# Differential attention stage: scores in two PSUM places instead of three, transposed groups in two banks instead of one

## The reference, cut to what matters

```
sc = einsum('bqhmd,bkhmd->bhmqk', q, k) * scale         # 4 heads, m = 0, 1, q and k of 32 dims
p  = softmax(where(key_chunk <= query_chunk, sc, -inf)) # chunks of 64 frames
a  = p[:, :, 0] - lam * p[:, :, 1]                      # difference of the two maps
o  = a @ v                                              # v of 64 dims
y  = rmsnorm(o) * g * (1 - lambda_init) * silu(gate)
```

## Time and profile before

| | us |
|---|---|
| median of 3 runs | 2056.37 (2056.11 to 2059.1) |
| the profiled execution | 2055.35 |
| its span, first to last instruction | 2053.6 |
| PE busy | 1873.9 (91%) |
| DVE busy | 1306.2 (64%) |
| ACT busy | 1083.0 (53%) |
| POOL busy | 604.1 (29%) |
| mean granted TensorE clock | 0.945 |

### The profile page before, as it was taken

How to read it: one execution, slowest core, us unless ns; L and a number is a source line. 1 busy time by engine, 2 the same in 40 slices (tenths; PEclk the granted TensorE clock), 3 DMA queues, 4 the chain that set the end, 5 groups by cost and what they waited for, 6 DMA issues and landing times.

```text
span 2053.6 us, 34304 instructions
## 1 busy us (share of the span) xinstructions
PE 1873.9 (91%) x11552; PEld 1579.8 (77%) x11552; DVE 1306.2 (64%) x2685; ACT 1083.0 (53%) x2406; POOL 604.1 (29%) x542
## 2 busy tenths in 40 slices
PE   6999998899999999999999959999788999989998
PEld 6999998678787878787878857777566666767886
DVE  7705887577777777777676832434477788754444
ACT  6321211566666666666666722433378989962221
POOL 0000000344444444444444500101145666650000
PEclk9999999999999999999999868999689999998999
DMA  6432113000010101010101021424710404016542
GB/s 217 105 72 62 66 66 108 13 8 25 7 25 6 26 5 26 5 26 5 26 5 26 4 75 56 130 74 131 169 28 16 98 18 99 7 39 234 181 144 82
DMA packets 121867, 129.29 MB, mean 63 GB/s; under 512 B 81936, under 2 KB 94992, under 8 KB 120464
## 3 DMA queue, kind: packets, MB, share of 16 engines
q1 hardware_dynamic: 121744, 127.86, 21.5%
HBM read 85.89 MB, written 41.94 MB: 62 GB/s over the span
## 4 chain that ended last, share of the span: by engine, by line
PE 68%; DVE 15%; issue 7%; ACT 5%; DMA 2%; POOL 2%; SPq 0%; DVEq 0%; POOLq 0%; ACTq 0%
PE ps L662 8%; PE ps L648 6%; PE ps L616 5%; PE ps L617 5%; PE ps L618 5%; PE ps L603 4%; PE ps L604 4%; PE ps L605 4%; DVE small L1503 4%; PE ps L896 3%; PE ps L897 3%; PE ps L898 3%; PE ps L636 2%; PE ps L637 2%; DVE ring L1363 2%
## 5 line engine op out<-in xcount | busy, mean ns | idle before, releaser
L1621 POOL TENSOR_TENSOR ring_r<-ring,sp_hi 128x512 fp32r<-128x512 f32 (+1 forms) x320 | 358.5, 1120 | 822.4 <-DVE sp_hi L1366 822.4
L662 PEld LDWEIGHTS ps<-v,ring 128*128 128x128 f32 x2176 | 298.8, 200 | 55.4 <-DVE acc L1383 22.8
L662 PE MATMUL ps<-v,ring 128*128 128x65 f32 x2176 | 298.2, 279 | 16.5 <-DVE acc L1383 10.2
L1009 ACT ACTIVATE ring<-ps 128x512 f32<-128x512 f32 (+1 forms) x320 | 170.5, 533 | 221.6 <-PE ps L637 165.6
L1363 DVE SCALAR_TENSOR_TENSOR ring<-ring,ps 128x512 f32<-128x512 f32 (+1 forms) x320 | 192.0, 600 | 34.8 <-ACT ring L1014 32.8
L603 PE MATMUL ps<-w_hl,ht_hi 128*128 128x256 f32 x768 | 213.5, 278 | 0.7 <-DVE w_hl L1244 0.6
L604 PE MATMUL ps<-w_hl,ht_hi 128*128 128x256 f32 x768 | 213.3, 278 | 0.0
L605 PE MATMUL ps<-w_hl,ht_lo 128*128 128x256 f32 x768 | 213.3, 278 | 0.0
L616 PE MATMUL ps<-ht_hi,w_hl 128*128 128x512 f32 x448 | 200.0, 446 | 13.3 <-DVE ring L1351 7.0
L1647 POOL TENSOR_TENSOR p<-p 128x1024 f32<-128x1024 f32 (+4 forms) x96 | 164.9, 1729 | 159.5 <-ACT p L1156 159.2
L1021 ACT ACTIVATE ring<-ps 128x512 f32<-128x512 f32 (+1 forms) x320 | 170.3, 532 | 60.5 <-PE ps L648 59.7
(11 more groups left out here) (186 smaller groups left out, 3954.3 us busy)
## 6 DMA issues: line engine op xcount, KB each, us to landing
w_raw<-in_w_narrow SPq DMA_DIRECT2D x18, 512.0 KB, 3.9
xb<-in_x SPq DMA_DIRECT2D x16, 512.0 KB, 4.1
gate_scr<-ring SPq DMA_DIRECT2D x64, 128.0 KB, 1.8
qk_scr<-w_hl SPq DMA_DIRECT2D x32, 256.0 KB, 3.4
gb<-gate_scr SPq DMA_DIRECT2D x16, 512.0 KB, 3.8
yb<-y_scr SPq DMA_DIRECT2D x16, 512.0 KB, 4.7
xr<-in_x SPq DMA_DIRECT2D x16, 512.0 KB, 4.3
out_y<-ob SPq DMA_DIRECT2D x16, 512.0 KB, 2.9
```

Source lines behind the costliest of these rows:

```text
L662: mm = pe.matmul(ps[:, 4 + i % 2, j * (HD + 1):(j + 1) * (HD + 1)], ring[:, 4 + i % 2, j * P:(j + 1) * P], v1[:, kb, :], start=True, stop= ...
L1621: nc.gpsimd.tensor_tensor(ring_r[:, i % 4, j0 * P:], ring[:, i % 4, j0 * P:], sp_hi[:, i % 4, j0 * P:].bitcast(F32), ALU.subtract).then_in ...
```

## The change

Three places in one edit: the scores use places j % 2 (banks 0 to 3) and TensorE waits for the exponential of the unit two before; the transposed groups alternate between banks 4 and 5 and wait for the copy of the group two before; the turn-back keeps bank 6 to itself and waits for VectorE's reading of the turn-back before.

```diff
         def df_ps(j):
-            return psf[:, (j % 3) * KEYS:(j % 3 + 1) * KEYS]
+            return psf[:, (j % 2) * KEYS:(j % 2 + 1) * KEYS]
...
-                if U >= 3:
-                    pe.wait_ge(df_e, U - 2)
+                if U >= 2:
+                    pe.wait_ge(df_e, U - 1)
                 for g in range(-(-keys // TQ)):
                     w = min(TQ, keys - g * TQ)
-                    mm = pe.matmul(ps[:, 2 * (j % 3) + g, 0:w], df_q[u][:, m, row * P:(row + 1) * P],
+                    mm = pe.matmul(ps[:, 2 * (j % 2) + g, 0:w], df_q[u][:, m, row * P:(row + 1) * P],
                                    df_k[u][:, m, first + g * TQ:first + g * TQ + w], start=True, stop=True)
                 if first + keys == (row + 1) * P:
-                    mm = pe.matmul(ps[:, 2 * (j % 3) + g, w - P:w], ident_b[:], df_mask_qk[:], start=False, stop=True,
+                    mm = pe.matmul(ps[:, 2 * (j % 2) + g, w - P:w], ident_b[:], df_mask_qk[:], start=False, stop=True,
                                    skip_group_check=True)
...
                 pe.wait_ge(df_a, 3 * s + (1 if end <= 8 else 2 if end <= big else 3))
-                if g == 0 and s >= 3 and s % 2:
-                    pe.wait_ge(df_ob, (s - 1) // 2)
-                elif G:
-                    wait_evac(G - 1)
+                if G >= 2:
+                    wait_evac(G - 2)
                 for n in range(GROUPS[g]):
-                    mm = pe.transpose(ps[:, 6, n * P:(n + 1) * P], p1[:, s % 3, ...], ident[:])
+                    mm = pe.transpose(ps[:, 4 + G % 2, n * P:(n + 1) * P], p1[:, s % 3, ...], ident[:])
...
                 pe.wait_ge(df_oc, b + 1)
-                wait_evac((2 * b + 3) * N_GR - 1 if 2 * b + 3 <= N_SL else N_SL * N_GR - 1)
+                pe.wait_ge(df_ob, b)
...
-                nc.scalar.activation(at[:, G % 3, 0:w], ps[:, 6, 0:w], ACT.Copy).then_inc(df_at_a, 1)
+                nc.scalar.activation(at[:, G % 3, 0:w], ps[:, 4 + G % 2, 0:w], ACT.Copy).then_inc(df_at_a, 1)
...
-                nc.vector.tensor_copy(at[:, G % 3, 0:w], ps[:, 6, 0:w]).then_inc(df_at_d, 1)
+                nc.vector.tensor_copy(at[:, G % 3, 0:w], ps[:, 4 + G % 2, 0:w]).then_inc(df_at_d, 1)
```

More of the change, by code:

```diff
@@ L825, in df_turn @@
                 pe.wait_ge(df_a, 3 * s + (1 if end <= 8 else 2 if end <= big else 3))
-                if g == 0 and s >= 3 and s % 2:
-                    pe.wait_ge(df_ob, (s - 1) // 2)
-                elif G:
-                    wait_evac(G - 1)
+                if G >= 2:
+                    wait_evac(G - 2)
                 for n in range(GROUPS[g]):
-                    mm = pe.transpose(ps[:, 6, n * P:(n + 1) * P], p1[:, s % 3, (first + n) * P:(first + n + 1) * P], ident[:])
+                    mm = pe.transpose(ps[:, 4 + G % 2, n * P:(n + 1) * P], p1[:, s % 3, (first + n) * P:(first + n + 1) * P], ident[:])
                 mm.then_inc(df_t, 1)
```

## The result

The changed kernel takes 2240.26 us, median of 4 runs (2232.22 to 2255.99), against 2057.73 for the kernel before in the same comparison: ratio 1.0898, 95% interval 1.0871 to 1.0925. Forecast were 2257 us with a range of 2165 to 2345. The profiled execution took 2232.22 us, the fastest of the four, with a span of 2230.4, 176.8 more than before.

The account below looks back on a forecast made before the run. TensorE and ScalarE, both near full, were taken to bound the stage. From 2055.35 us, 134 for the longer step loop and first two steps plus 68 for the lower clock gave 2257 us, range 2165 to 2345.

Parts of the forecast that it names:

- The reading of the step: Three places let scores 2 start 2.64 us before their two-place release, scores 4 some 2.3 us before exponential 2 is done.
- Transposes in two banks, zero: Transposes' waits for copies, at most 23.7 us, can go; priced at zero because TensorE is left idle anyway.
- The ring, +134: Scores in two places close a loop: mean step 15.4 us against 11.10, +129 over 30 steps, +5 in the first two.
- The clock, +68: Long TensorE gaps lower the clock for about 5 us; 2.25 us lost per step, 68 us in 30 steps.
- item 7: TensorE's gap-free run from scores 4 to the end of group 4: 3.80 us, reaching 12.29 in the walked step.
- Signs to look for: Stage: score waits over 100 us, copy waits near zero, joined-minimum waits beyond 80, clock 0.50 after gaps, alternating 15 to 18 us period.
- First two steps, +5: First two steps, without transposes: exponentials 2 and 5 come 1 to 1.5 us later each, +5 us.
- Rival A: The clock holds through the stage and only the longer step costs: 2055 + 134 = 2189 us; chance 0.22.
- B: The clock stays low for the whole stage: 2055 + 323 = 2378 us; chance 0.08.
- C: Faster: the third place was slack and all 23.7 us of copy waits go, 2032 us; chance 0.04.
- D: Shorter loop: copy and weighings run beside TensorE's run from scores 4; step 13.2 us, +63, 2118 us; chance 0.08.
- item 8: After TensorE's run: copy of group 4 0.42, weighings 1.33, exponential 5 with its read 0.87; step closes at 14.9 us.

Follow-up runs that it names:

- the scores' half alone: Kernel before with scores in two places; transposed groups and turn-back stay in bank 6 with their old waits: 2230.91 us, ratio 1.0845.
- the kernel with the fills: Changed kernel plus idle identity transposes before the waits of scores 4 (16) and scores 2 (8 in even steps, 4 in odd): 2185.85 us, ratio 1.0625.
- the moved copy of group 4: Changed kernel with ScalarE's copy of group 4 moved behind weighings 1 and 2 and exponential 5: 2224.84 us, ratio 1.0821.
- one wait alone: Kernel before, three places, two runs: only unit 4 waits for exponential 2, 2144.45 us; only unit 2 waits for exponential 0, 2132.89 us.
- the late variance: Kernel before with VectorE's variance moved from behind minimum 3 to behind minimum 5, ScalarE's root to the step's end: 2039.11 us, ratio 0.9916.
- the reordered kernel: Changed kernel, same instructions in another order on TensorE, VectorE and ScalarE (scores 3 directly behind scores 2, copies and take later): 2132.21 us, ratio 1.0371.

## Why the prediction was right, by its steps

- *The reading of the step* was right: it is the third place that lets scores 2 and 4 start 2.6 and 2.3 us ahead of their release, and waits on just these two units cost as much as the change, though with a shorter ring and more time at the lower clock.
- *Transposes in two banks, zero:* right, shown by the scores' half alone.
- *The ring, +134:* measured 129 with the clock held up, and item by item within 1.1 us in the step shown above. At full clock odd steps took 14.6 us for a walked 14.9, even ones 15.4 for a walked 15.8, and the take's share was 0.8 for 0.94. The difference to the step before came out better than either side: the 11.10 it was held against contains steps 2 to 4, slow at the lower clock, and the steps behind them took 10.87 on average, so the one side was 0.3 us too long and the other 0.2. That these cancel is luck. The walk also calls its step odd with k = 4; as k = s % 8, a step with k = 4 is even. It took the sizes of one step and the order of the other, which did no harm, since odd steps of all k lay within 14.5 to 14.9.
- *The clock, +68:* measured 45 to 56, so this term was 12 to 23 us too large; it is the one that was mis-sized. The time at the lower clock was nearly as assumed (131 us in 30 steps, 4.4 each, against 5, and some 13 of them were there before). What was too high is its price. The prediction let every microsecond behind the gap cost half of one, as if all of it stood on the path; the changed kernel has 121 us more of it than the one with the fills and is 48 us longer in these steps (504.3 against 456.0), 0.4 us for each. And it comes in stretches of up to 13 us in some steps and none in others. The gap before scores 4 is where it fell in 19 of 29 cases, but filling the one before scores 2 gave nearly as much. That picture, one gap behind which item 7 slows down, fell, though its size nearly held.
- *Signs to look for:* score waits over 100 us (152.9), copy waits near zero, a lower clock, a period of 15 to 18 us that alternates (means of 15.8 in odd and 17.8 in even steps): as said. "ScalarE's waits for the joined minimum beyond 80" was wrong: they stayed at 30.2. ScalarE meets the wait earlier in its queue, at the copies of groups 0, 2 and 4, 165.2 us. The wait is written to the first instruction in the queue that it hits. Step 2, with the memset, lost 8.7 us against a mean of 5.7, which the prediction had ruled out; 12 us at the lower clock fell into it, so the memset's part is not known.
- *First two steps, +5:* measured 4.0. *The total:* +202 forecast, +183 measured.
- *Rival A* (clock holds, 2189) did not come by itself; the kernel with the fills, which is held to its condition, measured 2186. *B, C and D* did not come. Part of D's mechanism, item 8 run beside item 7, was tried as the moved copy of group 4 and gave 16 us, where I expected 39: behind ScalarE's tail a second way of nearly the same length (scores 0, minimum 0) closes the ring. The walk had mentioned it ("fits before") without its margin.

What stays open: how the loss of one wait alone splits, beyond the few steps at full clock; what the waits of units 0, 1, 3 and 5 cost; and which of two waits the late variance won its 16 us from.

## What to carry to other kernels

When a ring of buffers is cut, walk the closed loop through every engine's fixed order, and note the second longest way beside it: it decides what repairing the first is worth. Check the walk against single steps at full clock, since two terms off in opposite directions can give the right total. New gaps on TensorE can have a second price in its clock (here those of 1.7 to 3.8 us), which belongs in the sum of every variant, and a cheap test of that price is to fill them with idle matmuls. Before a second buffer is bought for a wait, look at what makes the copier late: here a four-element operation in the wrong place, behind which two engines waited.

## What the runs showed of the hardware

- Idle matmuls made the kernel 45 to 56 us faster by keeping the granted clock at 0.99 instead of 0.86 in the stretch 1540 to 1820 us. I had not expected that filling either of two gaps alone gives over half of that (43 and 35 us). In the reordered kernel the same means raised the clock from 0.95 to 0.99 and gave nothing: what the lower clock costs depends on whether TensorE is what the step waits for.
- A VectorE `tensor_scalar` of 128x4 f32 in SBUF took 0.17 us where it met none of GpSimd's additions and 2.09 us (the median of 16) in the kernel before, beside them, ending with them in the rows above. Where it met the last part of an addition it took 0.4 to 1.1 us. The page "SBUF — State Buffer" of the Trainium skill, section "SBUF: two separate sides", says that VectorE in a two-port mode and GpSimd share a port pair that whichever starts first holds for its whole instruction, while the other blocks; the two rows agree with it.
